# Low parts of 45 weight entries by accumulating DMAs, and one more seven-product step in 11 groups of two transformer blocks in fp32r

## What is computed

```python
def first_block(x, ...):
    h = rmsnorm(x, g_mix)                      # conv, attention, gates, w_mix_out: left out
    ...
    h = rmsnorm(x, g_mlp)
    u = jnp.square(jax.nn.relu(h @ w_ff1))     # w_ff1: 2048 x 8192
    x = x + u @ w_ff2                          # w_ff2: 8192 x 2048
    return rmsnorm(x, g_final)

def second_block(x, ...):
    ...                                        # attention with a bias, pools, w_out: left out
    return x + conv_ffn(rms_norm(x, ffn_norm_g), w_up, conv_w, conv_b, w_down)

def conv_ffn(h, w_up, conv_w, conv_b, w_down): # w_up: 2048 x 11264, w_down: 5632 x 2048
    u = h @ w_up
    y = conv_b + causal depthwise conv of width 3 over tokens (u, conv_w)
    gate, val = jnp.split(y, 2, axis=-1)
    return (jax.nn.silu(gate) * val) @ w_down
```

## Time and profile before

| | |
|---|---|
| median of 3 runs | 2369.18 us (2367.63 to 2369.34) |
| the profiled execution | 2369.1 us, its span 2367.3 us |
| TensorE busy | 2362.3 us (100%), 12510 matmuls, granted clock 1.0 throughout |
| VectorE busy | 1787.1 us (75%) |
| ScalarE busy | 1292.2 us (55%) |
| POOL busy | 0.2 us |
| DMA | 452.17 MB, 191 GB/s, loads take 58.8% of the 16 engines' time |

### The profile page before, as it was taken

The page is one execution under the profiler, slowest core; times in us unless marked ns, Lnnn a source line. Parts: engine busy times, 40 slices in busy tenths (PEclk is TensorE's granted clock), DMA queues, the critical chain, the costliest instruction groups (busy, mean ns, idle before and its releaser), DMA issues.

```text
span 2367.3 us, 31012 instructions
## 1 busy us (share of the span) xinstructions
PE 2362.3 (100%) x12510; PEld 2023.8 (85%) x12510; DVE 1787.1 (75%) x1964; ACT 1292.2 (55%) x1512; POOL 0.2 (0%) x4
## 2 busy tenths in 40 slices
PE   9999999999999999999999999999999999999999
PEld 8888888888888888888888888888888888888887
DVE  5575666666877967967968777888778788897888
ACT  5454454554656555556556566556555555555554
POOL 0000000000000000000000000000000000000000
PEclk9999999999999999999999999999999999999999
DMA  7556556665665675665665555556555655565655
GB/s 253 163 176 200 158 196 193 192 191 171 203 203 171 223 231 171 214 197 184 213 195 190 185 187 169 169 178 198 184 187 186 205 177 188 187 221 187 189 173 183
DMA packets 238044, 452.17 MB, mean 191 GB/s; under 512 B 16570, under 2 KB 20780, under 8 KB 237772
## 3 DMA queue, kind: packets, MB, share of 16 engines
q1 hardware_dynamic: 237147, 449.07, 58.8%
q10 hardware_dynamic: 752, 1.12, 0.1%
HBM read 446.46 MB, written 3.67 MB: 190 GB/s over the span
## 4 chain that ended last, share of the span: by engine, by line
PE 99%; DVE 1%; DMA 0%; ACT 0%; issue 0%; ACTq 0%; DVEq 0%
PE PS L696 42%; PE PS L698 21%; PE PS L729 11%; PE PS L731 11%; PE PS L730 11%; PE PS L658 0%; PE PS L625 0%; PE PS L646 0%; PE PS L635 0%; PE PS L563 0%; DVE WL L1335 0%; DMA VR<-in_g_mix 0%; PE PS L708 0%; PE PS L647 0%; PE PS L626 0%; PE PS L552 0%
## 5 line engine op out<-in xcount | busy, mean ns | idle before, releaser
L1335 DVE TENSOR_TENSOR WL<-RAW,WH 128x1024 fp32r<-128x1024 f32 (+1 forms) x844 | 991.0, 1193 | 431.9 <-ACT WH L856 429.4
L696 PE MATMUL PS<-XHL,WH 128*128 128x512 f32 x3968 | 1248.2, 396 | 0.0
L856 ACT ACTIVATE WH<-RAW 128x1024 fp32r<-128x1024 f32 (+1 forms) x845 | 859.4, 1032 | 659.0 <-PE PS L698 455.1
L698 PEld LDWEIGHTS PS<-XHL,WL 128*128 128x128 f32 x3968 | 745.4, 188 | 176.0
L698 PE MATMUL PS<-XHL,WL 128*128 128x256 f32 x3968 | 779.8, 278 | 0.0
L696 PEld LDWEIGHTS PS<-XHL,WH 128*128 128x128 f32 x3968 | 605.1, 189 | 2.1 <-issue 1.0
L729 PE MATMUL PS<-WH,MHL 128*128 128x512 f32 x915 | 356.9, 390 | 0.0
L731 PE MATMUL PS<-WH,MHL 128*128 128x512 f32 x915 | 356.1, 389 | 0.0
L730 PE MATMUL PS<-WL,MHL 128*128 128x512 f32 x915 | 356.0, 389 | 0.0
L731 PEld LDWEIGHTS PS<-WH,MHL 128*128 128x128 f32 x915 | 171.7, 188 | 35.9
L730 PEld LDWEIGHTS PS<-WL,MHL 128*128 128x128 f32 x915 | 171.8, 188 | 35.1
(11 more groups left out here) (226 smaller groups left out, 1613.8 us busy)
## 6 DMA issues: line engine op xcount, KB each, us to landing
RAW<-in_w_ff SPq DMA_DIRECT2D x256, 512.0 KB, 4.2
RAW<-in_w_in SPq DMA_DIRECT2D x224, 512.0 KB, 3.9
RAW<-in_w_up SPq DMA_DIRECT2D x176, 512.0 KB, 4.5
RAW<-in_w_down SPq DMA_DIRECT2D x88, 512.0 KB, 4.3
RAW<-in_w_mix_out SPq DMA_DIRECT2D x32, 512.0 KB, 4.2
RAW<-in_w_out SPq DMA_DIRECT2D x32, 512.0 KB, 4.2
RAW<-in_w_conv_out SPq DMA_DIRECT2D x16, 512.0 KB, 3.6
RAW<-in_w_attn_out SPq DMA_DIRECT2D x16, 512.0 KB, 4.2
```

What stands on the lines that cost most here:

```text
L696: mm(PS[:, b + p.banks[j], :], h[:, k, j * P:(j + 1) * P], x[:, kc, :], start=st, stop=False)
L698: t = mm(PS[:, b + p.banks[j], 0:T], l[:, k, j * P:(j + 1) * P], x[:, kc, 0:T], start=False, stop=en)
L856: act(high, raw, AF.Copy).then_inc(*own.made(hi, i))
L1335: tt(low, raw, high.bitcast(f32), sub).then_inc(*own.made(lo, i))
```

## The change

Three things are changed. (1) GROUPS: each ff2 group and each down group of eight has one more seven-product step. The orders of steps go as follows (E and S in the order of work, first group / second group of a segment):

| | before | after |
|---|---|---|
| ff2 | E S E S E S E E / E E S E S S E E | E S S E S S E E / E S S E S S E E |
| down of 8 | E E E E S S E E / E E S E S S E E | E E E S S S E E / E S E S S S E E |
| down of 6 | E E E S E E / E E S S E E | unchanged |

There are seven ff2 groups and four down groups of eight, so 11 S more: with the groups of w_mix_out and w_out, which stay, 41 S become 52 and the matmuls of the groups 3045 - 33 = 3012. (2) For 45 entries, each the second half of an E, VectorE makes no low part. ScalarE writes the negated high part into a buffer of WLX (two buffers, `negative`, two entries ahead of its ordinary splits), and POOL issues a DMA that adds the weights from HBM to it (`accum_op=add`), which gives the low part. TensorE waits for `hi` of the entry and for this DMA. Taken are, as far as 7 entries lie between one and the next but one: in ff2 steps 0, 3, 6 and 7 of a first group (counted from 0) and 3, 6 and 7 of a second; in down of eight 0, 1, 6, 7 and 2, 6, 7; in down of six 0, 1, 4, 5 and 4, 5. (3) Memory: AXH and AXL get a fourth slot, AS moves into TC, WLX takes 2 x 1024 columns; because of it BIAS is loaded later (after the last ff2 group; GF stays) and masked at the start of the first Q stage.

```diff
@@ -15,11 +15,13 @@
 AHEAD = NS - 1
+APART = 7
+ADDED, ADDED_FROM = ("ff", "down"), 1
 WARM = 8
 ER_STEP = 16
 UNIT = 1024
-GROUPS = {"ff": (((0, 1, 2, 3, 4, 5, 6, 7), (1, 3, 5)), ((0, 2, 1, 4, 3, 5, 6, 7), (2, 4, 5))),
-          "down8": (((0, 1, 2, 4, 3, 5, 6, 7), (4, 5)), ((0, 2, 1, 4, 3, 5, 6, 7), (2, 4, 5))),
+GROUPS = {"ff": (((0, 1, 2, 3, 4, 5, 6, 7), (1, 2, 4, 5)), ((0, 1, 2, 3, 4, 5, 6, 7), (1, 2, 4, 5))),
+          "down8": (((0, 1, 2, 4, 3, 5, 6, 7), (3, 4, 5)), ((0, 1, 2, 4, 3, 5, 6, 7), (1, 3, 4, 5))),
...
@@ -345,11 +347,10 @@
-            AXH = sb("AXH", [P, 3, 4, P], f32r, c=c)
-            AXL = sb("AXL", [P, 3, 4, P], f32r, c=c)
-            AS = sb("AS", [P, 4, P], c=c)
-            sb("QK2pad", [P, 512], c=c)
+            AXH = sb("AXH", [P, 4, 4, P], f32r, c=c)
+            AXL = sb("AXL", [P, 4, 4, P], f32r, c=c)
             GF = sb("GF", [P, D], c=c)
+            WLX = sb("WLX", [P, 2, UNIT], f32r, c=c)
...
@@ -364,6 +365,7 @@
+        AS = TC[:, :, 2:2 + P]
...
@@ -424,6 +427,8 @@
             _, per, n = units[u] if what != "b22" else (None, 1, 512)
+            if buf is WL and e in added:
+                return WLX[:, added[e] % 2, 0:per * n].rearrange("p (k n) -> p k n", k=per)
             return buf[:, e % NS, 0:per * n].rearrange("p (k n) -> p k n", k=per)
...
@@ -443,9 +448,31 @@
 
+        item_of = {it.key: it for it in items}
+        added, last_two = {}, [-APART, -APART]
+        for it in items:
+            for n, st in enumerate(it.steps):
+                if it.args["u"][0] in ADDED and not st.seven:
+                    for ent in st.ents[ADDED_FROM:]:
+                        if ent - last_two[0] >= APART and ent - last_two[1] >= 2:
+                            added[ent] = len(added)
+                            last_two = [last_two[1], ent]
+        added_ents = list(added)
+        BIAS_UNIT = ents[item_of["ff2", 3, 2].parts[0].ent][1] + AHEAD + NR + 4
+        added_before_bias = max((e for e in added if e < item_of["ff2", 3, 2].parts[0].ent), default=None)
+        first_added_mix = min((e for e in added if e < item_of["ff", 0, 0].parts[0].ent), default=None)
+        first_added_wo = min((e for e in added if e > item_of["Q", 0].end), default=None)
+
+        def low_landed(e):
+            n = added[e]
+            return s_low[n % 2], 16 * (n // 2 + 1)
+
+
         raw_free = {}
         for e, (what, u) in enumerate(ents):
-            if what == "unit":
+            if e in added:
+                raw_free[u] = hi, e
+            elif what == "unit":
...
@@ -522,12 +548,16 @@
                 if i == BIAS_AFTER:
+                    own.wait_ge(*used[branches_end])
+                    e.dma_start(GF[:], io["g_final"].rearrange("(a n) -> a n", a=1).to_broadcast([P, D])
+                                ).then_inc(s_gf, 16)
+                if i == BIAS_UNIT:
                     own.wait_ge(s_er, er_all)
                     own.wait_ge(*used[branches_end])
+                    if added_before_bias is not None:
+                        own.wait_ge(*used[added_before_bias])
                     e.dma_start(BIAS[:], bass.AP(ERD.tensor, ERD.offset + P - 1, [[8 * 384 - 1, P], [384, 8], [1, T]])
                                 ).then_inc(s_wp, 16)
-                    e.dma_start(GF[:], io["g_final"].rearrange("(a n) -> a n", a=1).to_broadcast([P, D])
-                                ).then_inc(s_gf, 16)
             for g in range(2):
...
@@ -535,6 +565,12 @@
+
+        def gpsimd(e):
+            own = Own(e, None)
+            for i, n in added.items():
+                own.wait_ge(*negated[i])
+                e.dma_start(wview(WL, i), units[ents[i][1]][0], accum_op=add).then_inc(s_low[n % 2], 16)
 
...
@@ -740,7 +776,11 @@
                         for half, ent in enumerate(st.ents):
-                            own.wait_ge(*lo[ent])
+                            if ent in added:
+                                own.wait_ge(*hi[ent])
+                                own.wait_ge(*low_landed(ent))
+                            else:
+                                own.wait_ge(*lo[ent])
                             h, l = wview(WH, ent), wview(WL, ent)
...
@@ -844,6 +884,8 @@
                     what, u = ents[i]
+                    if i + 2 in added:
+                        negative(i + 2)
                     raw, high, _ = pieces(i)
...
@@ -856,6 +898,17 @@
 
+            def negative(i):
+                u, n = ents[i][1], added[i]
+                own.wait_ge(*landed(u))
+                if n >= 2:
+                    own.wait_ge(*used[added_ents[n - 2]])
+                if i == first_added_mix:
+                    own.wait_ge(*used[item_of["conv", 3].end])
+                if i == first_added_wo:
+                    own.wait_ge(*masked[2, 1])
+                act(wview(WL, i), raw_view(u), AF.Copy, scale=-1.0).then_inc(*own.made(negated, i))
+
...
@@ -1331,8 +1384,9 @@
                     raw, high, low = pieces(i)
-                    own.wait_ge(*hi[i])
-                    tt(low, raw, high.bitcast(f32), sub).then_inc(*own.made(lo, i))
+                    if i not in added:
+                        own.wait_ge(*hi[i])
+                        tt(low, raw, high.bitcast(f32), sub).then_inc(*own.made(lo, i))
                     if what == "left":
...
@@ -1948,11 +2002,10 @@
                     e.memset(TC[:, :, 0:2], 0.0).then_inc(*own.made())
-                elif it.key == ("ff", 3, 1):
+                elif it.key == ("Q", 0):
                     chain()
                     own.wait_ge(s_wp, 16)
                     tt(BIAS[:], BIAS[:], over4(M, 8), add).then_inc(*own.made())
-                elif it.key == ("Q", 0):
                     chain()
...
```

More of the change, by code:

```diff
@@ L389, in build @@
         s_id, s_gm, s_vr, s_const, s_rel = (sem(n) for n in ("s_id", "s_gm", "s_vr", "s_const", "s_rel"))
+        s_low = [sem("s_low0"), sem("s_low1")]
         s_er, s_wp, s_gf = sem("s_er"), sem("s_wp"), sem("s_gf")
@@ L402, in build @@
             signals("used used_half gm_up vec_up rel_up turned spread_up logf_up run_up scores probs_up mix_up norm_up"))
-        hi, x_hi, part_hi, sum_hi, copied, squared, root, gate, tap, exps, probs, placed, softplus, cr_hi, square_hi, pair1, rooted, act_step = (
-            signals("hi x_hi part_hi sum_hi copied squared root gate tap exps probs placed softplus cr_hi square_hi pair1 rooted act_step"))
+        hi, x_hi, part_hi, sum_hi, copied, squared, root, gate, tap, exps, probs, placed, softplus, cr_hi, square_hi, pair1, rooted, negated, act_step = (
+            signals("hi x_hi part_hi sum_hi copied squared root gate tap exps probs placed softplus cr_hi square_hi pair1 rooted negated act_step"))
         lo, t13_made, t_made, x_lo, square_lo, summed, summing, left, evacuated, scaled, multiplied, tapped, mean, column, diagonal, row = (
@@ L494, in build @@
         rel_all, er_all = 48, 16 * 16
-        item_of = {it.key: it for it in items}
         BIAS_AFTER = ents[item_of["ff", 1, 0].parts[0].ent][1] + AHEAD - 1 + NR
@@ L1062, in pair_sums @@
                     own.wait_ge(*used[sum_used[i]])
-                act(AXH[:, i], AS[:], AF.Copy).then_inc(*own.made(sum_hi, (u, i)))
+                act(AXH[:, i], AS, AF.Copy).then_inc(*own.made(sum_hi, (u, i)))
                 free["TA"] = summed, (u, i)
@@ L1650, in pair_sums @@
                 own.wait_ge(*sum_hi[u, i])
-                tt(AXL[:, i], AS[:], AXH[:, i].bitcast(f32), sub).then_inc(*own.made(summed, (u, i)))
+                tt(AXL[:, i], AS, AXH[:, i].bitcast(f32), sub).then_inc(*own.made(summed, (u, i)))
             def sums_x(it):
@@ L1986, in vector @@
             work.flush()
-        for engine in (tensor, vector, scalar, sync):
+        for engine in (tensor, vector, scalar, gpsimd, sync):
             engine(Counting())
@@ L2006, in _ @@
             vector(nc.vector)
+        @block.gpsimd
+        def _(eng):
+            gpsimd(nc.gpsimd)
         @block.tensor
```

## The result

The changed kernel takes 2436.18 us (median of 4 runs, 2433.25 to 2438.16) against 2369.20 us before: the ratio is 1.0283, with a 95% interval of 1.0265 to 1.0301. That is 67 us lost where 16 were forecast; the direction was right, the size was not. The profiled execution took 2433.25 us around a span of 2431.5.

What follows compares the result with a forecast made beforehand. TensorE was taken as the bound, with VectorE nearly a second one in the groups. 7.5 us won against 22 or so of new waits gives +15, one late DMA makes it +16: 2385 us, range 2367 to 2432.

Steps and rivals of the forecast that it cites:

- 33 x 0.2267 = 7.48 us: All groups: eleven more S save 3 matmuls each, 7.48 us in all if TensorE never waits.
- ff2 first groups, 0.8 at the third step: ff2 first groups, third step, now S: TensorE waits 0.8 us for the low part of its third piece.
- about 0.3 us to spare: ff2 first groups: after an E with one low part left out, the next S pair holds with about 0.3 us.
- down first groups, "4.3 us" and "5.0": First down groups of eight, three S in a row: waits of 4.3 us, and 5.0 in the last segment.
- ff2 second groups, "2.2 us": ff2 second groups: half sums fall between the first two S; the second S's low parts come 2.2 us late.
- down second groups, "late by 1.6": Second down groups of eight: of three S in a row, the third is late by 1.6 us.
- Sum with DMAs in time: Whole kernel, DMAs always in time: 7.5 us won, 22 or so of new waits, +15 us.
- Halfway is 7.2: Accumulating DMA of 512 KB takes 7.2 us, between bounds 4.2 and 10.2; one is late by 0.9: +16 in total.
- 45 negations ... behind each there is a split with lead: ScalarE: 45 negations at 1.03 us, costed at nothing but for +0.3 in the first down pair.
- Faster: VectorE's relief reaches the places where it is late, TensorE never waits: 2361.7 us; chance 0.09.
- Descriptors starved: Descriptor writing waits for VectorE gaps, a DMA takes 15 us or so: over 2520 us; chance 0.03.
- Accumulation late: DMAs over 9 us, 22 E steps wait: 2406 us at 9, 2428 at 10.2; chance 0.27, 0.08 beyond 2432.

Runs made afterwards that it cites:

- run 1: Changed kernel with the new orders alone: no accumulating DMA, every low part on VectorE; 2403.81 us, ratio 1.0155.
- run 7: New orders without accumulations, VectorE making the previous group's half sums ahead of the pair sums for the second group's first S; 2399.54 us, ratio 1.0135.
- run 6: Orders of before, all low parts on VectorE, no POOL DMA, but ScalarE makes 49 negations that nobody reads; 2394.44 us, ratio 1.0113.
- run 10: Orders of before, low parts left out by the same rule, negations in place, POOL's DMAs plain copies instead of accumulations; 2379.36 us, ratio 1.0050.
- run 3: Changed kernel with POOL's 45 DMAs as plain copies into WLX instead of accumulations; 2420.15 us, ratio 1.0227.
- run 2: Changed kernel with the orders of before, accumulating DMAs by the same rule (49 of them); 2390.80 us, ratio 1.0099.
- run 5: Orders of before, accumulating DMAs only for the second half of the first step of each of the 13 groups; 2386.76 us, ratio 1.0075.
- run 9: Orders of before, accumulating DMAs only for the second half of the first step of the seven first groups; 2367.58 us, ratio 0.9999.

## Why the prediction was wrong in size

The direction and the first link (VectorE late at an S) were right. Three terms failed: the negations, put at nothing, cost 12 to 27 us by themselves; the first S of a second group waits for PSUM banks, which the sum left out; and the accumulating DMA, put at 7.2 us, takes 9.1. The lower clock behind long waits, in no term, comes on top.

- **"33 x 0.2267 = 7.48 us" won**: right, 12477 matmuls against 12510.
- **ff2 first groups, 0.8 at the third step**: right. Run 1 has 0.83 there, and 0.8 more at the sixth step, for which the "about 0.3 us to spare" counted on a low part left out that run 1 doesn't leave out.
- **down first groups, "4.3 us" and "5.0"**: right, 4.3 and 5.1 us in run 1. Three S in a row cost just what the durations of VectorE's operations say.
- **ff2 second groups, "2.2 us"**: the step that failed among the orders. I put the half sums between the first S and the second and asked when *low parts* are ready. But the first S itself can't begin before the half sums are done, since it writes the banks they read. Run 1 has 5.3 to 5.5 us in these groups, three times, of which the wait at the first S is 3.1 to 3.3 and the lower clock behind it 1.7. The same holds for the down second groups, "late by 1.6": their step with that lateness shows 1.6 and 1.3, but the first S adds 2.6 and 4.5. Sum with DMAs in time: +15 forecast, +36 for the orders by run 1, which makes the low parts that the forecast left out; no run has the new orders with those low parts gone, the DMAs in time and nothing held up, so the size of the error is not known more exactly. Every S of before in a second group is its third step or later, so no row of before shows this wait; the wait for the banks is in the code all the same.
- **The clock** was no term at all. In the kernel before it is 1.00 throughout, and no wait of TensorE's there is over 1.0 us. Runs 1 and 7 put some 7 us on it for the orders, and the changed kernel has 8.6.
- **"Halfway is 7.2"** for the accumulating DMA: measured 8.8 us from the issue, 9.1 from the end of the negation, 5.8 to 11.3 by place. The bounds, 4.2 and 10.2, held the median though not the longest; the midpoint was too low. With 8.1 us of time and 9.1 of need, the tight places decide, as the prediction had said that they do "from 8 us on": 18 waits of TensorE where it counted 22. The formula of the Trainium skill (DMA: Bandwidth & Descriptors, "Anatomy of one DMA") is for DMAs that GpSimd issues; by it the estimate for 512 KB is 3.2 us. Neither row of such a DMA agrees, with the raw loads under way beside them: POOL's copy takes 5.7 us (3.8 at the least), the accumulation 8.8.
- **"45 negations ... behind each there is a split with lead"**: wrong: +26.9 us for the negations alone with all low parts on VectorE (run 6), +12 with VectorE relieved (run 10), and in the new orders up to 16 (run 3 against run 1). It is not additive to the late DMAs. I had looked at how long a negation takes (1.04 us, as costed) and not at what it waits for. The prediction even says that "raw loads will land later" and costs that at nothing, because ScalarE seldom waited for them: true of splits, which ask for their raw load two entries later than the negations do.
- **Rivals.** Faster: nowhere. Descriptors starved (over 2520): no; POOL's DMAs landed in 8.8 us with VectorE 85% busy. Accumulation late: it happened, with the price per place that it gave, beside the forecast's own waits and not in their stead. At 9.1 us its line gives some 2408; for the other 28 us the runs have the banks, the clock and the negations' hold, without a price of each in the changed kernel. The chance of 0.08 for a time beyond 2432 was meant for a landing over 10.2 us; that is not what happened.

What stays open is how the changed kernel's 67 us divide. Added one after the other, the orders are 36 us (run 1), the negations with copies 16 more (run 3) and the accumulation in place of the copy another 16 (the changed kernel); in another order the shares would differ, since on the orders of before the hold with copies is 12 and both together 23 (runs 10 and 2). No run takes away the hold and keeps all the DMAs.

## What to carry to other kernels

For an operation put into an in-order queue, its duration is the smaller question. Ask what it waits for, and whether the work behind it in that queue was ready earlier: a 1 us operation that waits 4 us for a load due later delays everything behind it, on other engines too. When a step is moved to the front, list all that its *first* instruction waits for, buffers and PSUM banks included, and not only its inputs. And where an engine has no wait at all, price a new wait above its length: here 0.3 us for each restart, and 1.7 us of lower clock behind many of those of 1.9 us and more.

## What the runs showed of the hardware

- An accumulating DMA of 512 KB from HBM onto SBUF, issued by POOL beside the raw loads, lands 8.8 us after its issue (median; 5.8 to 11.3); in the second groups of run 5, where there is one such DMA per group, in 5.9 to 6.2. A copy by the same queue lands in 5.7, a load by SP's queue in 4.4. POOL is occupied for 1.20 us by issuing the accumulation and for 0.72 by the copy.
- The granted clock, 1.00 for the whole kernel before, fell to 1.2 GHz behind long waits of TensorE (2.7 and 3.3 us in the rows above, 1.9 and 2.0 in run 6) for about eight matmuls, 1.7 us a time in the two rows above. Not behind each: a wait of 3.0 us in the changed kernel (at 1164.57) and one of 2.3 us in run 1 left it at 1.00. In run 7 no wait is over 1.6 us, and it stays at 1.00.
- 24 MB of accumulating traffic raise the DMA share of the groups from about 0.60 to 0.7, and SP's raw loads of w_ff land in 4.5 us instead of 4.2. What this traffic costs by itself no run shows: run 9, which loses nothing, has only seven of these DMAs.
